# Recurrence levels spread through the value and gate products, and the head finish moved under later products

## The reference, cut to what matters

```python
proj = einsum('bld,de->ble', h, w_in)          # 5 parts of 1024: q, zf, zb, v, g
lf_f, k_f = gates(zf, lb[0]); lf_b, k_b = gates(zb, lb[1])
o_f, s_f = chunk_scan(q, lf_f, k_f, v, s0_f)   # decayed scores times v, plus the state's part
o_b, s_b = chunk_scan(flip(q), flip(lf_b), flip(k_b), flip(v), s0_b)
o = rmsnorm_per_head(o_f + flip(o_b)) * norm_g * silu(g)
out = o @ w_out
```

## Time and profile before

| what | value |
|---|---|
| median of 3 runs | 1149.44 us (1145.53 to 1153.17) |
| the profiled execution, its own time | 1146.26 us |
| its span, first to last instruction | 1144.1 us |
| TensorE busy | 959.1 us (84%) |
| VectorE, ScalarE, GpSimd busy | 248.3, 222.6, 147.7 us |
| mean granted TensorE clock | 0.928 |

### The profile page before, as it was taken

The page is one execution under the profiler, slowest core; times in us unless marked ns, Lnnn a source line. Parts: engine busy times, 40 slices in busy tenths (PEclk is TensorE's granted clock), DMA queues, the critical chain, the costliest instruction groups (busy, mean ns, idle before and its releaser), DMA issues.

```text
span 1144.1 us, 21357 instructions
## 1 busy us (share of the span) xinstructions
PE 959.1 (84%) x8838; PEld 569.0 (50%) x8839; DVE 248.3 (22%) x554; ACT 222.6 (19%) x473; POOL 147.7 (13%) x243
## 2 busy tenths in 40 slices
PE   3799987999986898799799999379968999888770
PEld 2466455766454645455355555165444555444430
DVE  1100157200157225110000101341340101000005
ACT  1111101211101203022122222230131222211112
POOL 0000000100000101112111222120012221211112
PEclk9899988999988899799999999789978999998995
DMA  9975400585413433999999999560361999999954
GB/s 386 396 291 229 188 37 3 212 345 225 170 54 150 187 126 138 410 425 426 423 428 425 427 424 405 206 264 0 110 273 68 373 380 425 427 426 426 426 235 165
DMA packets 34186, 318.44 MB, mean 278 GB/s; under 512 B 6788, under 2 KB 9284, under 8 KB 16080
## 3 DMA queue, kind: packets, MB, share of 16 engines
q1 hardware_dynamic: 23024, 297.67, 63.1%
q0 software_dynamic: 7840, 15.18, 3.5%
q10 hardware_dynamic: 3264, 4.72, 1.1%
HBM read 309.19 MB, written 17.33 MB: 285 GB/s over the span
## 4 chain that ended last, share of the span: by engine, by line
PE 62%; DMA 24%; DVE 4%; issue 4%; ACT 3%; POOLq 1%; SPq 0%; POOL 0%; ACTq 0%; DVEq 0%
DMA ring<-in_moe_w_up 16%; PE ps L789 15%; PE ps L533 11%; PE ps L536 7%; PE ps L669 7%; PE ps L806 6%; DMA work<-hrow,gi 4%; PE ps L467 3%; DMA ring<-in_w_mod 2%; PE ps L573 2%; PE ps L753 1%; PE ps L701 1%; PE ps L512 1%; PE ps L684 1%; ACT ring L870 1%
## 5 line engine op out<-in xcount | busy, mean ns | idle before, releaser
L789 PE MATMUL ps<-ring,work 128*64 128x256 f32 x2432 | 293.2, 396 | 36.2 <-DMA ring<-in_moe_w_up 33.7
L789 PEld LDWEIGHTS ps<-ring,work 128*64 128x64 f32 x2432 | 185.7, 142 | 143.0 <-issue 49.2
L806 PE MATMUL ps<-ring,work 128*64 128x512 f32 x608 | 145.3, 598 | 0.0
L533 PE MATMUL ps<-ring 128*128 128x384 f32 x384 | 129.2, 495 | 5.2 <-ACT ring L870 5.2
L1274 DVE TENSOR_TENSOR work<-work,ps 128x128 f32<-128x128 f32 x76 | 21.9, 288 | 375.5 <-ACT work L963 375.5
L533 PEld LDWEIGHTS ps<-ring 128*128 128x128 f32 x384 | 72.9, 193 | 56.0 <-ACT ring L870 5.3
L536 PE MATMUL ps<-ring 128*128 128x512 f32 x192 | 89.8, 621 | 0.7 <-issue 0.7
L669 PE MATMUL ps<-ring 128*128 128x512 f32 x192 | 84.6, 602 | 1.2 <-DVE ring L1349 0.7
L467 PE MATMUL ps<-ring,scond 128*2 128x128 f32 x1536 | 50.3, 287 | 20.9 <-DMA ring<-in_w_mod 20.9
L806 PEld LDWEIGHTS ps<-ring,work 128*64 128x64 f32 x608 | 40.3, 136 | 55.2 <-issue 44.1
L669 PEld LDWEIGHTS ps<-ring 128*128 128x128 f32 x192 | 37.0, 194 | 47.8 <-issue 45.9
(11 more groups left out here) (155 smaller groups left out, 742.7 us busy)
## 6 DMA issues: line engine op xcount, KB each, us to landing
ring<-in_moe_w_gate SPq DMA_DIRECT2D x32, 2048.0 KB, 20.4
ring<-in_moe_w_up SPq DMA_DIRECT2D x32, 2048.0 KB, 27.2
ring<-in_moe_w_down SPq DMA_DIRECT2D x32, 2048.0 KB, 29.1
ring<-in_w_mod SPq DMA_DIRECT2D x24, 2048.0 KB, 10.3
ring<-in_hgrn_w_in SPq DMA_DIRECT2D x10, 2048.0 KB, 12.2
ring<-yrows SPq DMA_DIRECT2D x6, 1024.0 KB, 6.9
ring<-in_hgrn_w_out SPq DMA_DIRECT2D x2, 2048.0 KB, 7.8
ring<-in_fourier_w_out SPq DMA_DIRECT2D x2, 2048.0 KB, 17.6
```

The lines of the kernel that those rows point to most:

```text
L533: last = mm(bank[:, 0:T], W[:, k, c * P:(c + 1) * P], hT[:, k, :], start=(k == 0), stop=(k == KD - 1))
L789: last = mm(ps[h * SLOTS:(h + 1) * SLOTS, GU_BANK[j], 0:2 * P], xt[:, k % 4, k // 4 * SLOTS:(k // 4 + 1) * SLOTS], Wgu[:, :, at:at + P], s ...
L806: last = mm(ps[h * SLOTS:(h + 1) * SLOTS, Y_BANK, :], hidT[:, j, q * SLOTS:(q + 1) * SLOTS], slot_d(S[2])[:, 2 * q + j, h * C512:(h + 1) * ...
```

## The change

The 7 levels of a half are cut into small pieces, each behind one matmul of the value and gate groups. A small level now scores only the columns that it needs (16 of 32), forward and backward into one bank, and VectorE takes them with one masked copy (6 copies a half instead of 11). Half 0's finish is spread over groups 0 to 6 of half 1; half 1's finish is spread over the output product, which runs over the first four heads' k first. To make room in PSUM, projections rotate over two banks instead of four, and modulation units use one bank and (from unit 7) one ring slot. SP loads a w_in unit when TensorE has finished with its slot (before: when ScalarE had), and no longer holds unit 12. Semaphore waits, banks and the order of out_project in both layers follow from it; ScalarE and VectorE get the same pieces in the new order.

```diff
         def mod_slot(U):
...
+            return [3, 4, 5, 2, 3, 2, 3][U] if U < 7 else 2 if U < 20 else [2, 0, 1, 2][U - 20]
...
+        STREAM = ([("mod", U) for U in range(4)] + [("hgrn", 0), ("hgrn", 1), ("mod", 4), ("mod", 5), ("mod", 6),
+                  ("mod", 7), ("hgrn", 2), ("mod", 8), ("hgrn", 3), ("mod", 9), ("mod", 10), ("hgrn", 4), ("mod", 11),
+                  ("hgrn", 5), ("mod", 12), ("hgrn", 6), ("mod", 13), ("mod", 14), ("hgrn", 7), ("mod", 15),
+                  ("mod", 16), ("hgrn", 8), ("mod", 17), ("mod", 18), ("hgrn", 9), ("mod", 19), ("hgrn", 10),
+                  ("mod", 20), ("hgrn", 11)])
+        LEVEL_AT = [4 + 6 * i for i in range(len(SIZES))]
+        OUT_ORDER = [0, 1, 3, 2, 4, 5]
...
-                if u == 12:
-                    sp.wait_ge(o_mm, 3)
...
             def project_half(half):
...
+                        if n >= 2:
+                            pe.wait_ge(proj_evac, n - 1)
+                        bank = ps[:, n % 2, :]
...
+                            if half == 1 and kind < 2:
+                                finish_heads(0, m, k)
+                            if m >= 12:
+                                step = 8 * (m - 12) + k
+                                if step in (1, 2, 3):
+                                    diagonal_scores(half, step - 1)
+                                i, at = divmod(step - LEVEL_AT[0], 6)
+                                if 0 <= i < len(SIZES) and at in (0, 1, 3, 4):
+                                    level_scores(half, i, at // 3, at % 3)
...
+                        if m % 2 == 1 and m < 16:
+                            mod_next(4 + 8 * half + m // 2)
...
+            def finish_heads(half, m, k):
+                if (m, k) == (0, 1):
+                    turn_keys(half, 0)
+                    turn_keys(half, 1)
+                if (m, k) == (0, 5):
+                    increment(half, 0)
+                    turn_keys(half, 2)
+                if (m, k) == (1, 2):
+                    increment(half, 1)
+                    turn_keys(half, 3)
+                if (m, k) == (1, 5):
+                    outputs(half, 0)
...
+            def level_scores(half, i, d, part):
...
+                to = lambda a: a.rearrange("p (b two h) -> p b two h", two=2, h=h)[:, :, 1 - d, :]
+                for th in range(6 * part, 6 * part + 6):
+                    t, hh = divmod(th, HH)
+                    for g in range(4):
+                        a = hh * T + t * P + g * SMALL
+                        last = mm(to(ps[g * SMALL:(g + 1) * SMALL, 5 + n % 2, th * SMALL:(th + 1) * SMALL]),
+                                  kd[d][:, a:a + SMALL], to(qd[d][:, a:a + SMALL]), start=True, stop=True)
...
+            def finish_and_project():
+                part = lambda n, k0, k1: out_part(0, oT, "hgrn", 10, n, range(k0, k1))
...
+                pe.wait_ge(proj_evac, 36)
+                turn_keys(1, 0)
+                turn_keys(1, 1)
+                part(0, 0, 2)
+                increment(1, 0)
+                turn_keys(1, 2)
+                part(0, 2, 4)
+                increment(1, 1)
+                turn_keys(1, 3)
+                outputs(1, 0)
+                part(1, 0, 2)
+                increment(1, 2)
+                part(1, 2, 4)
+                increment(1, 3)
...
+                part(2, 0, 3)
+                outputs(1, 1)
+                part(2, 3, 4)
+                outputs(1, 2)
+                turn_outputs(1, 0)
+                pe.wait_ge(oT_ready, 4)
+                part(0, 4, 8)
+                turn_outputs(1, 1)
+                pe.wait_ge(oT_ready, 5)
+                part(1, 4, 8)
+                turn_outputs(1, 2)
...
+                part(3, 0, 8)
...
+                part(2, 4, 8)
...
+                part(4, 0, 8)
+                part(5, 0, 8)
```

More of the change, by code:

```diff
@@ new lines, in diagonal_scores @@
+            def diagonal_scores(half, t):
+                if t == 0:
+                    pe.wait_ge(proj_evac, 18 * half + 12)
+                for h in range(HH):
+                    o = (t * HH + h) * SMALL
+                    for g in range(4):
+                        a = h * T + t * P + g * SMALL
+                        for d in range(2):
+                            last = mm(ps[g * SMALL:(g + 1) * SMALL, 5, o:o + SMALL], kd[d][:, a:a + SMALL],
+                                      qT[:, a:a + SMALL], start=(d == 0), stop=(d == 1))
+                if t == TT - 1:
+                    last.then_inc(diag_mm, 1)
@@ new lines, in increment @@
+            def increment(half, j):
+                t, d = UNITS[j]
+                pe.wait_ge(kT_ready, 4 * half + j + 1)
+                if j == 0:
+                    pe.wait_ge(off_copied, half + 1)
+                if j >= 2:
+                    pe.wait_ge(s_ready, 4 * half + j - 1)
+                for h in range(HH):
+                    last = mm(ps[:, 2 + j % 2, h * P:(h + 1) * P], kT[:, j % 2, h, :],
+                              vrow[:, t, h * P:(h + 1) * P], start=True, stop=True)
+                last.then_inc(u_mm, 1)
@@ new lines, in outputs @@
+            def outputs(half, t):
+                if t == 0:
+                    pe.wait_ge(score_ready, 4 * (half + 1))
+                if t == 1:
+                    pe.wait_ge(kT_ready, 4 * half + 4)
+                    pe.wait_ge(s_ready, 4 * half + 4)
+                for h in range(HH):
+                    a = h * T + t * P
+                    out = ps[:, O_BANK[t], h * P:(h + 1) * P]
+                    last = mm(out, score[:, t, h, :], vrow[:, t, h * P:(h + 1) * P], start=True, stop=(t == 0))
+                    if t:
+                        st_f = s0[:, 0, h, :] if t == 1 else s1[:, 0, h, :]
+                        st_b = s1[:, 1, h, :] if t == 1 else s0[:, 1, h, :]
+                        mm(out, qd[0][:, a:a + P], st_f, start=False, stop=False)
+                        last = mm(out, qd[1][:, a:a + P], st_b, start=False, stop=True)
+                last.then_inc(o_mm, 1)
@@ L842, in _ @@
             pe.wait_ge(z_evac, KD)
[L843 removed]
+            out_project_fourier()
             turn_norm("m1", 1)
```

528 lines of the change are left out of this document (268 added, 260 removed).

## The result

| what | before | after |
|---|---|---|
| median of the runs | 1151.31 us (4 runs) | 1121.61 us (4 runs, 1118.09 to 1121.93) |
| ratio of after to before, 95% interval | | 0.974 [0.9693, 0.9787] |
| profiled execution, own time; span | 1146.26; 1144.1 us | 1121.53; 1119.7 us |
| mean granted TensorE clock | 0.928 | 0.94 |

The profiled execution came 24.7 us down, against 28.7 forecast by the sum; the median is within 2 us of the predicted 1120. That it came so near is partly luck: before, the profiled execution lies 5 us under its median, after it lies on it, and the 2.4 us that the forecast put on the sum made up for most of what was missed. The page's first part hardly differs from before: what TensorE works is nearly the same, the idle time around it went.

A forecast was written before the change was run, and what follows sets the result against it. The mixer stage was taken as bound by one engine at a time and by fetching short instructions. New price 40.6 + 15.2 + 19.8 + 8 = 83.6 us against 112.3, 28.7 less: 1117.6, put at 1120 us, range 1103 to 1140.

The forecast's parts named there:

- What goes away: Mixer levels and finishes of both halves: their old price, 112.3 us in all, is replaced by a new one.
- What the levels cost: Levels spread among value and gate groups: 20.3 us a half, 40.6 in both, including 6 x 1.82 and 4.9 of interruptions.
- 16 columns at nothing: Small level bursts: moving 16 columns instead of 32 saves nothing; ends 0 and 4.5 us a half.
- VectorE hidden: Levels: VectorE needs 5.8 us of a 7.7 us level period, so it stays hidden with 2 to 3 us to spare.
- Fetching: Level stretches: instruction blocks arrive late while weights load, 4 us a half, 8 in all; ends 0 and 28.
- The first rival: Level stretches: instruction blocks arrive in time, 8 us less, 1112 us (1103 if 16 columns also halve small bursts); chance 0.20.
- the second: Level stretches: every instruction block takes the loaded 6.66 us, 28 us instead of 8, 1140 us; chance 0.13.
- Half 0's finish: Spread over half 1's groups 0 to 6: 13.2 us of records plus 2.0 for 11 interruptions, 15.2, no wait.
- Half 1's finish: Between pieces of the output product: 13.2 us of records, 1.6 of interruptions, 5 of four waits, sum 19.8.
- From there on the same time: Behind the output product, through routing and experts to the end: time unchanged, so the gain passes through in full.
- The third rival: Value and gate groups: the clock falls to 0.57, 62 us more, 1182 us, slower than before; chance 0.07.
- The fourth: Finish hand-overs, 11 us idle before, reappear whole in half 1's groups and output product: 6 us more, 1126, inside forecast's range.

The follow-up runs named there:

- e7: Kernel after, but all level bursts of a half stand in one piece behind its last gate product; 1155.39 us, ratio to before 1.005.
- e4: Kernel after, but half 0's finish in one piece behind two products of half 1's first group; 1135.09 us, ratio to before 0.9867.
- e3: Kernel after, but all of half 1's finish in one piece ahead of the output product; 1129.33 us, ratio to before 0.9824.
- e5: Kernel after, but five weight units a half load only 128 of 4096 columns; stage 361.7 us against 368.6 (routing inputs differ).
- e2: Kernel after, but small-level scores move all 32 columns instead of 16; stage 369.1 us against 368.6 (routing inputs differ).
- e6: Kernel after plus three extra 2048 KB transfers a half, which nothing reads, through the level stretch; 1139.07 us, ratio to before 0.9917.
- e9: Kernel after with half 1's finish reordered against its remaining waits, short bursts kept; 1118.69 us, ratio to before 0.9732.
- e1: Kernel after, but small levels in 10 bursts of 96 records a half instead of 20 of 48; 1120.77 us, ratio to before 0.9752.
- e8: Kernel after with half 1's finish reordered and small levels in 10 bursts of 96 records a half; 1120.32 us, ratio to before 0.9742.
- e11: Kernel after with all level bursts behind the last gate product and weight units then moving cut to 128 columns; 1132.7 us, stage 396.2 us.

## Why the prediction was right

The forecast was met because its largest terms came where they were put and near their size, and because two errors of opposite sign partly cancelled: the levels with their fetching were 6.8 us dearer than priced, the finishes 4.1 us cheaper.

**What goes away.** Most idle time of levels and finishes went, and the clock rose to 0.98 to 1.00: half 0 ended at 187.3 (predicted near 185), half 1 at 348.9 (345), the output product at 408.0 (405). Where levels or finishes are put together again (e7, e4, e3), the hand-overs and fetch waits return.

**What the levels cost: mis-sized by 3 to 4 us a half.** The step "6 x 1.82" took a burst's price from one of 192 records, 9.5 ns each. e5, where fetching costs nothing, gives the bare price: 68.57 - 45.1 = 23.5 us in half 0 and 24.1 in half 1, against 20.3. By after's chain, a burst of 48 takes 0.53 and not 0.455 us (20 bursts: 1.5 more), a third of the diagonal, 64 records, 0.79 and not 0.61 (0.5 more), level 64 3.08 and not 2.6 (0.5), level 32 1.76 and not 1.9 (0.1 less), an interruption 0.19 and not 0.18 (0.3); the turn of a modulation row, 0.26, lies in these groups and was not counted. That is 3.0, of half 0's 3.2. A record costs more in a short burst (11.0 ns in one of 48) than in one of 192 (9.5), and most in the diagonal's 64 (12.3); why is not shown.

**16 columns at nothing** was right within 0.6 us a half (e2). **VectorE hidden** was right: TensorE does not wait for it at any level. A level's period, 133.06 to 143.19 us less the modulation unit's 1.86, is 8.3 us and not 7.7, for the larger burst price. In e7, with no products between, VectorE's 9.1 us (5.9 + 3.2) appear.

**Fetching: 8 us forecast, 7.8 measured** (e5 against after). The mechanism held, and e6 bears the direction out; that the size agrees to 0.2 us is luck. The working stood on a single block under load, and the term left out that the clock falls behind some waits, which is 1.7 of the 7.8 (half 1's) and in e6 nearly half of what was lost beyond after (4.5 and 3.6 of 9.5 and 7.4). The first rival (no fetch loss, 1112 us) fell with e5 and e6; the second (every block loaded, 1140) is about where e6 lies, 1139.07, with a DMA share of 0.55 instead of 0.4. Its mechanism is real and its condition was not met; that the figures agree is chance, since half of e6's loss is clock, which that rival does not hold.

**Half 0's finish: over-sized by 2.0 us**, exactly the step that priced 11 interruptions at 0.18. The groups took 87.80 us with 87.70 busy, so no wait, as said; what was wrong is that an interruption costs the same whatever cuts in. Turns, increments and outputs are tiles of 128 x 128 like the products around them, and they cost 0.11 a record and nothing more (`0.22 PE ps L668 x2` in the chain of e9). The 0.19 belongs to changes between whole tiles and narrower ones. It is not the number of moving columns: a modulation unit (L468) moves 128 like the finish, but on tiles of 128 x 2, and the two products behind it take 1.05 us again. The Trainium skill, in TensorEngine Tiling (Array Packing), section "Key Properties", says that a change of tiling mode drains the engine; both the price of one and the absence of the other agree with it.

**Half 1's finish: 17.7 against 19.8.** The same 1.6 of interruptions is missing; the four waits, forecast as 0.7, 1.5, 2 and 0.7, were 0.8, 1.2, 1.3 and 0.7 (2.0 in two): 4.0 against 5, in the places named. So this finish was over-sized by the same step and by 1 us of waits.

**From there on the same time:** 2 us came back in this trace, which is no more than the stretch behind the stage varies by where its work is the same (707.8 us in e6, 710.5 in e1, 713.5 in e8; 709.75 before, 711.7 after). 1.3 of it lie in the routing. The chain there, at the logits' products:

```profile
425.52 0.43 PE ps L794 x2
```

Before, four such records took 0.44 us, so two 0.22, here 0.43: the lower of the two clock levels, for 3.7 us instead of 2.3. That is about the routing's 1.3. These products took 2.1 us in e1, e3 and e5 to e8, but 3.5 in e4 and e9; what decides it was not tested, so that the change makes it is not shown.

**The third rival (clock falls, 1182)** did not come: 1.00 and 0.98 in the level stretches. Its mechanism exists: e6 shows it behind waits of 2.2 to 3.2 us, for a few us each, e7 in most of its packed levels, and in after there was one such place. **The fourth (waits move along, 1126)** came only in part: 4.0 of the 11 us, where the forecast had 5. e3 and e4 show more of it.

## What to carry to other kernels

Many short matmuls cost in three ways when packed: the fetch of the program, the hand-overs between levels, and the clock. Spread in small bursts behind long products, the hand-overs are hidden and the fetch nearly so, and the price is about 0.2 us for each change of tile shape. Price a burst from one of its own length, and a change of shape only where the shape changes. When weights are moved into such a stretch, add what the fetch loses to them: here about 4 us a half at a DMA share of 0.4 and, by one trace, three times that at 0.55.

## What was not expected of the hardware

- Spread bursts with idle queues lost nothing to fetching (e5), packed ones with idle queues 21.3 us in 14 waits (e11), one packet of 16 KB coming every 3.4 to 3.9 us. For spread bursts the load is the whole loss.
- A fetch wait of 3.21 us was followed by products at half the clock: four records took 3.78 us instead of 1.91 (e6).
- A burst of 48 records takes 0.53 us with 16 columns and 0.56 with 32: 11.0 and 11.7 ns a record, against 9.5 with 32 columns in a burst of 192.
- Small products in the shape of their neighbours cost no interruption that shows: 116 records in 11 places took 13.2 us, 0.114 each, as in one piece.
